# Two edits to a two-block kernel: 32 weight slots of the second block as three fp32r products, and the second norm's root moved behind the gate and up products

## The reference, cut to what matters

```python
# first block, each of 2 layers (D_FF = 2816)
h = h + jnp.concatenate([attn_out, conv_out], axis=-1) @ w_out[l]
hn = rmsnorm(h, norm2_g[l])
gate, up = jnp.split(hn @ w_gate_up[l], 2, axis=-1)
h = h + (jax.nn.silu(gate) * up) @ w_down[l]
...
# second block, one layer
h = _rms(x, g_mix) * (1.0 + sc1) + sh1
proj = h @ w_in     # gq gk gv gz gb ga | dil_q dil_k dil_v | gate_a gate_b
y_a = gated_deltanet(gq, gk, gv, gz, gb, ga, ...)
y_b = dilated_mixture(dil_q, dil_k, dil_v, ...)
merged = sigmoid(gate_a) * (y_a @ w_up_gdn) + sigmoid(gate_b) * (y_b @ w_up_dil)
x = x + gt1 * (merged @ w_out)
h2 = _rms(x, g_ffn) * (1.0 + sc2) + sh2
x = x + gt2 * moe_ffn(h2, ...)      # 64 experts, 8 for each token, and one shared
```

## Time and profile before

| | us |
|---|---|
| median of 3 runs | 1879.63 (1878.8 to 1880.18) |
| the profiled execution, its time | 1879.7 |
| its span in the trace | 1877.9 |
| TensorE busy | 1789.8 (95%) |
| VectorE busy | 826.2 (44%) |
| ScalarE busy | 595.0 (32%) |
| mean granted TensorE clock | 0.981 |

### The profile page before, as it was taken

How to read it: one execution, slowest core, us unless ns; L and a number is a source line. 1 busy time by engine, 2 the same in 40 slices (tenths; PEclk the granted TensorE clock), 3 DMA queues, 4 the chain that set the end, 5 groups by cost and what they waited for, 6 DMA issues and landing times.

```text
span 1877.9 us, 29645 instructions
## 1 busy us (share of the span) xinstructions
PE 1789.8 (95%) x11720; PEld 1392.1 (74%) x11720; DVE 826.2 (44%) x1587; ACT 595.0 (32%) x1100; POOL 55.7 (3%) x48
## 2 busy tenths in 40 slices
PE   7988999989989999799999999999999999999997
PEld 5767999977779999677888878887555555555554
DVE  4956555449666554376644373115222222222222
ACT  2244444311354443365521242203122222222221
POOL 0010000000010000005100000000000000000000
PEclk9999999999999999899999999998999999999999
DMA  6533445545344555332412323346799999999992
GB/s 271 220 125 146 139 176 179 181 154 203 138 161 151 181 188 194 115 123 92 130 46 90 122 103 112 134 148 241 277 392 395 399 396 402 395 398 398 391 401 98
DMA packets 63951, 403.97 MB, mean 215 GB/s; under 512 B 13056, under 2 KB 14592, under 8 KB 15232
## 3 DMA queue, kind: packets, MB, share of 16 engines
q1 hardware_dynamic: 63440, 401.34, 56.0%
q10 hardware_dynamic: 432, 1.51, 0.2%
HBM read 401.39 MB, written 1.44 MB: 215 GB/s over the span
## 4 chain that ended last, share of the span: by engine, by line
PE 87%; DVE 9%; ACT 3%; issue 1%; DMA 0%; SPq 0%; DVEq 0%; ACTq 0%
PE ps L826 22%; PE ps L1377 19%; PE ps L935 13%; PE ps L629 6%; PE ps L1351 5%; PE ps L1367 4%; DVE big L2098 2%; DVE inv L2321 2%; PE ps L1294 1%; PE ps L1268 1%; PE ps L585 1%; PE ps L1319 1%; PE ps L1277 1%; PE ps L1359 1%; PE ps L877 1%
## 5 line engine op out<-in xcount | busy, mean ns | idle before, releaser
L935 PE MATMUL ps<-hn,ring 128*128 128x256 f32 x1152 | 267.4, 385 | 3.6 <-ACT hn L1690 3.6
L935 PEld LDWEIGHTS ps<-hn,ring 128*128 128x128 f32 x1152 | 216.9, 193 | 36.4 <-issue 9.3
L826 PE MATMUL ps<-xhi,wlo 128*128 128x272 f32 (+1 forms) x800 | 227.5, 284 | 0.0
L826 PE MATMUL ps<-xhi,whi 128*128 128x272 f32 (+1 forms) x800 | 227.0, 284 | 0.0
L2161 DVE TENSOR_TENSOR wlo<-ring,whi 128x2048 fp32r<-128x2048 f32 x76 | 174.1, 2291 | 116.6 <-ACT whi L1560 116.6
L826 PE MATMUL ps<-hn_lo,whi 128*128 128x272 f32 (+1 forms) x672 | 192.3, 286 | 0.0
L1377 PE MATMUL ps<-big 128*64 128x512 f32 x816 | 181.8, 594 | 0.0
L1377 PE MATMUL ps<-ring,big 128*64 128x512 f32 x816 | 181.7, 594 | 0.0
L1560 ACT ACTIVATE whi<-ring 128x2048 fp32r<-128x2048 f32 x76 | 145.1, 1909 | 79.2 <-PE ps L826 78.8
L629 PE MATMUL ps<-hn,ring 128*128 128x272 f32 x640 | 159.3, 405 | 8.9 <-DVE hn L2069 5.6
L629 PEld LDWEIGHTS ps<-hn,ring 128*128 128x128 f32 x640 | 122.9, 195 | 41.3 <-issue 16.5
(11 more groups left out here) (399 smaller groups left out, 2628.9 us busy)
## 6 DMA issues: line engine op xcount, KB each, us to landing
ring<-in_stream SPq DMA_DIRECT2D x277, 1024.0 KB, 5.0
big<-in_stream SPq DMA_DIRECT2D x102, 1024.0 KB, 9.6
h<-in_xT SPq DMA_DIRECT2D x1, 1088.0 KB, 5.1
out_xT<-h SPq DMA_DIRECT2D x1, 1024.0 KB, 4.7
big<-in_consts ACTq DMA_DIRECT2D x1, 896.0 KB, 4.7
cst<-in_consts SPq DMA_DIRECT2D x1, 576.0 KB, 6.0
big<-in_consts ACTq DMA_DIRECT2D x1, 326.5 KB, 5.1
from_blocks<-big SPq DMA_DIRECT2D x1, 256.0 KB, 2.0
```

The source lines that it names most:

```text
L826: m = mm(out, a[:, at_:at_ + P], b[:, k, kept], start=first and i == 0, stop=last and i == 2)
L935: m = mm(ps[:, i % 2, n * T:(n + 1) * T], a, b, start=k == 0, stop=k == DC - 1)
```

## The change

It has two parts.

In the first block `normalize` is no longer called for the second norm. As each chunk of h gets w_out's result, VectorE multiplies it by the gain alone, ScalarE rounds it into `hg_hi` (a buffer of its own) and VectorE subtracts. TensorE still forms the sums of squares behind w_out (six chunks of squares, then two), then goes on to gate/up with the unscaled activation. VectorE multiplies both the gate and the up result by the reciprocal of the root, out of PSUM, for each of the 22 slots; ScalarE's silu then reads the scaled gate from SBUF.

In the second block the 32 slots from dq0 to UG3 are split like those of the first block: ScalarE rounds the slot into one of two buffers `wb` (`high_of`), VectorE subtracts into the ring of `wlo` (`low_of`), and each product is three fp32r matmuls. The activations `hm`, `yo` and `yb` are split as well; the low half of `hm` takes the place of `hm`. Buffers of the stretch move: the values of the dilated heads into pieces, `kbg`, `vn`, `sqy`, `dS` and `dpT` elsewhere. ScalarE's scaling of the keys for the state (`keys_scaled(gK, 96)`) moves from before the triangular inversion to behind it.

```diff
@@ TensorE, first block
-                    if c % 4 == 0:
-                        W(pe, "sq_ready", 2 * which + c // 4 + 1, l)
+                    if c in (0, 6 if which else 4):
+                        W(pe, "sq_ready", 2 * which + (c > 0) + 1, l)
...
@@ TensorE, second block
+            def both_of(name):
+                d = at(name) - SPLIT
+                W(pe, "wlo_ready", d + 1, DEPTH)
+                return wb[d % 2], wlo[(B2 + at(name)) % RING]
...
+                    pairs = [(hi, hm_hi), (lo, hm_hi), (hi, hm_lo)]
...
+                    for j, (w, x_) in enumerate(pairs):
+                        ...
+                        m = mm(ps[:, i % 2, n * T:(n + 1) * T], a, b, start=k + j == 0, stop=k == DC - 1 and j == len(pairs) - 1)
@@ ScalarE, first block
+                def high_part(c):
+                    W(act, "hn_ready", DC + c + 1, l)
+                    f(hg_hi[c][:, kept], hnf[:, c, kept], ACT.Copy).then_inc(xhi_ready, 1)
+                for n in range(3):
+                    high_weights(3 + n)
+                    high_part(2 * n)
+                    high_part(2 * n + 1)
+                f(sq[:, 0:6, kept], h[:, 0:6, kept], ACT.Square).then_inc(sq_ready, 1)
+                high_part(6)
+                high_part(7)
+                f(sq[:, 6:8, kept], h[:, 6:8, kept], ACT.Square).then_inc(sq_ready, 1)
                 root_of_mean(l, 1, small[:, 60:61])
-                for c in range(DC):
-                    W(act, "hn_ready", DC + c + 1, l)
-                    f(xhi[:, c, kept], hnf[:, c, kept], ACT.Copy).then_inc(xhi_ready, 1)
...
-                    f(sgu[:, i % 2, kept], ps[:, 2 * (i % 2), kept], ACT.Silu).then_inc(gate_act, 1)
+                    W(act, "gate_scaled", 2 * n + 1, l)
+                    f(sgu[:, i % 2, kept], sgu[:, i % 2, kept], ACT.Silu).then_inc(gate_act, 1)
@@ ScalarE, second block
+            def high_of(name):
+                i = ORDER.index(name)
+                act.wait_ge(ring_full[(B2 + i) % RING], ((B2 + i) // RING + 1) * 16)
+                if i == SPLIT:
+                    act.wait_ge(tu_full, 8)
+                elif i == SPLIT + 1:
+                    act.wait_ge(w_full, 4)
+                else:
+                    landed(ORDER[i - 2])
+                f(wb[(i - SPLIT) % 2][:, :], ring[:, (B2 + i) % RING, :], ACT.Copy).then_inc(whi_ready, 1)
...
@@ in dil_in(name), behind the copies (gate_out(j) likewise)
+                high_of(ORDER[i + 2])
@@ VectorE, first block
+                    W(dve, "h_added", 1 + n + 1, l)
+                    v.tensor_scalar(hnf[:, n, kept], h[:, n, kept], par[:, PN2 + n:PN2 + n + 1], None, ALU.mult).then_inc(hn_ready, 1)
...
-                normalize(l, 1, par[:, PN2:PN2 + DC], hnf)
...
+                    v.tensor_tensor(sgu[:, i % 2, kept], ps[:, 2 * (i % 2), kept], inv[:, 0, kept], ALU.mult).then_inc(gate_scaled, 1)
+                    v.tensor_tensor(up_r[i % 2][:, kept], ps[:, 2 * (i % 2) + 1, kept], inv[:, 0, kept], ALU.mult).then_inc(gate_scaled, 1)
@@ VectorE, second block
+            def low_of(name):
+                i = ORDER.index(name)
+                j = (B2 + i) % RING
+                W(dve, "whi_ready", i - SPLIT + 1, DEPTH)
+                v.tensor_tensor(wlo[j][:, :], ring[:, j, :], wb[(i - SPLIT) % 2][:, :], ALU.subtract).then_inc(wlo_ready, 1)
...
+            low_of("dk2")
             dil_norm("dq2")
             value_rest(2)
+            low_of("dv0")
             dil_norm("dk0")
             next_state(2)
+            low_of("dv1")
             dil_norm("dk1")
             value_rest(3)
...
             dil_weights(0)
+            low_of("ek0")
             dil_norm("eq0")
             dil_mask(1)
+            low_of("ek1")
             dil_norm("eq1")
             y_norm(1)
             dil_weights(1)
...
-            for d in range(4, 8):
-                dil_mask(d)
-                dil_weights(d)
+            low_of("G0")
+            dil_mask(4)
+            low_of("G1")
+            dil_weights(4)
+            low_of("G2")
+            dil_mask(5)
+            low_of("G3")
+            W(dve, "xhi_ready", 2, DEPTH)
+            v.tensor_tensor(yo_lo[:, :, :], yo, yo_hi[:, :, :], ALU.subtract).then_inc(xlo_ready, 1)
+            dil_weights(5)
+            low_of("G4")
+            low_of("G5")
+            dil_mask(6)
+            dil_weights(6)
+            low_of("G6")
+            low_of("G7")
+            dil_mask(7)
+            dil_weights(7)
```

More of the change, by code:

```diff
@@ L80 @@
 OUT2 = len(ORDER)
+SPLIT = ORDER.index("dq0")
 EX0 = B2 + OUT2 + 4
@@ L206, in build @@
         xhi, hn_lo, cat_lo, hff_hi, hff_lo = (rounded[n] for n in ("xhi", "hn_lo", "cat_lo", "hff_hi", "hff_lo"))
+        hg_hi = [rounded["hg_hi"][:, c, :] for c in range(DC - 1)] + [rounded["hg_hi7"][:, 0, :]]
+        up_r = [zpad[:, c, PAD:] for c in range(2)]
         ps = ctx.enter_context(nc.psum_tensor("ps", [P, 8, 512], F32))
@@ L295, in build @@
         flat = ps[:, :, :].rearrange("p a b -> p (a b)")
+        wb = [rounded[f"wb{j}"] for j in range(2)]
+        hm_hi, hm_lo = rounded["hm_hi"], xhi[:, :, 0:T]
+        yo_hi, yo_lo, yb_hi, yb_lo = (rounded[n] for n in ("yo_hi", "yo_lo", "yb_hi", "yb_lo"))
         COUNT = {}
@@ L825, in product @@
                     for i, (a, b) in enumerate(((w[0], hi), (w[1], hi), (w[0], lo))):
-                        m = mm(out, a[:, at_:at_ + P], b[:, k, kept], start=first and i == 0, stop=last and i == 2)
+                        b = b[k] if b is hg_hi else b[:, k, :]
+                        m = mm(out, a[:, at_:at_ + P], b[:, kept], start=first and i == 0, stop=last and i == 2)
                     return m
@@ L1259, in up_gdn @@
                 i, bank = at(name), UP_BANK[name]
-                w = slot(B2 + i, 0).rearrange("p (k n c) -> p k n c", k=8, n=2)
+                hi, lo = (w.rearrange("p (k n c) -> p k n c", k=8, n=2) for w in both_of(name))
                 if name == "UG0":
-                    pe.wait_ge(ya_ready, 4)
+                    W(pe, "xlo_ready", 2, DEPTH)
                     pe.wait_ge(mroot, len(SUMS))
@@ L1984, in _ @@
             dil_y_out(7)
+            act.wait_ge(yb_ready, 8)
+            f(yb_hi[:, :, :], yb, ACT.Copy).then_inc(xhi_ready, 1)
             act.dma_start(w_r, w_router_d).then_inc(loaded2, 16)
             act.dma_start(cst3, consts3_d).then_inc(loaded2, 16)
+            for name in ("UD0", "UD1", "UG2", "UG3"):
+                high_of(name)
             token_squares(2, lambda g: 8 + 4 * g + 4)
@@ L2525, in next_state @@
                 m.then_inc(s_ready, 1)
+            low_of("dq1")
             value_rest(0)
+            low_of("dq2")
             dil_norm("dq0")
             next_state(0)
+            low_of("dk0")
             value_rest(1)
+            low_of("dk1")
             dil_norm("dq1")
             next_state(1)
+            low_of("dk2")
             dil_norm("dq2")
             value_rest(2)
+            low_of("dv0")
             dil_norm("dk0")
             next_state(2)
+            low_of("dv1")
             dil_norm("dk1")
             value_rest(3)
+            low_of("dv2")
             dil_norm("dk2")
+            low_of("eq0")
+            low_of("eq1")
             dil_mask(0)
+            low_of("eq2")
             y_norm(0)
             dil_weights(0)
+            low_of("ek0")
             dil_norm("eq0")
             dil_mask(1)
+            low_of("ek1")
             dil_norm("eq1")
@@ L2553, in _ @@
             dil_weights(2)
+            low_of("ev1")
             dil_norm("ek1")
             dil_mask(3)
+            low_of("ev2")
             dil_norm("ek2")
@@ L2585, in _ @@
             merge(1)
+            low_of("UG3")
             times_dil(1)
```

118 lines of the change are left out of this document (72 added, 46 removed).

## The result

The changed kernel takes 1858.03 us (median of 4 runs, 1856.76 to 1858.69) against 1879.22 for the kernel before on the same chip (1877.32 to 1880.18). The ratio is 0.9888, with a 95% interval of 0.9871 to 0.9905: faster by 21.2 us where 18.6 were forecast, and inside the range of 1850 to 1871. The profiled execution took 1858.68 us, with a span of 1856.9.

The account below looks back on a forecast made before the run. TensorE was taken as the bound in the changed stretches, except eq0 to ev1, where it waits for VectorE; transfers set the pace in the last third. 1879.7 - 12.0 - 16.8 + 10.2 = 1861.1 us, range 1850 to 1871.

Parts of the forecast that it names:

- The first block's turn: From w_out to the second gate slot: waits and half clock go, gaining 6.5 us in layer 0, 5.5 in layer 1.
- Rival (d): First block: the first gate slot still waits for halves or squares, so only -6.6 us, 1873 us; chance 0.04.
- The scales at no cost: Gate/up loop: VectorE's iteration with the scales takes 5.45 us, fitting slots of 5.7 or 6.0 us; cost nothing.
- Rival (e): Gate/up loop: the scales make VectorE the bound, iterations over 6.3 us; slower, 1886 us at 6.6; chance 0.06.
- Slots of 5.7 us: Second block, dq0 to UG3: three fp32r products replace each fp32 one, 1.2 us less a slot, 38.4 over 32 slots.
- the walk: Second block: the three engines' queues followed from dq0 to UG3, giving a lead of 16.8 us before the clock's cost.
- The walk from eq0 to G7: Second block: longer TensorE waits for VectorE; lead 8.8 us at eq0, 5.1 at turn 3, 9.6 at UG0.
- Rival (b): Second block: waits shorter than in the walk and the clock stays up, 1851 us; chance 0.10.
- VectorE sets the pace: From eq0 to ev1: VectorE's work makes cycles of 22.8, 22.3 and 22.8 us; TensorE's shorter slots buy nothing.
- The clock: Second block: half clock behind TensorE's longer waits, counted as six at 1.7 us, costs 10.2 us.
- Rival (c): Second block: clock stays down as long as in layer 0, seven waits at 3.0 return 21 us, 1872; chance 0.14.
- The sum: Whole kernel: 1879.7 less 12.0 (first block) and 16.8 (second block), plus 10.2 (clock), gives 1861.1 us.

Follow-up runs that it names:

- the part alone: The kernel before with the first block's edits alone; 1871.35 us, ratio 0.9945.
- turns later: The changed kernel with each dil_turn one slot later in TensorE's order and dil_out(7) behind UG0; 1834.85 us, ratio 0.9775.
- weights first: The changed kernel with VectorE's dil_weights(d) ahead of y_norm(d), for d of 0 to 3; 1845.71 us, ratio 0.982.
- both orders changed: The changed kernel with VectorE's dil_weights ahead of y_norm and each dil_turn one slot later on TensorE; 1835.93 us, ratio 0.9778.
- the waits filled: The changed kernel with 164 useless fp32r products on TensorE ahead of dil_turn 0, 1, 2, 3 and 7; 1849.97 us, ratio 0.9841.

## Why the prediction was right

**The first block's turn: right, within 0.6 us.** The second slot comes 9.7 and 9.12 us after the sums began (9.8 and 9.5 expected), with no wait and the clock at 1.00. The gains at the place are 6.7 and 5.9, 12.6 in all, for 12.0, and the profile of the part alone shows the same two. That its times came to 10.3 only is put down to the scatter around them, which is not shown run by run. In the whole kernel the lead of 6.6 us had shrunk to 4.75 at layer 1's sums; behind the wait of 2.71 us in the unchanged norm that opens the layer, the low clock lasted longer than before, and the second profile of the same kernel, 1.9 us ahead at those sums, shows this as scatter. Rival (d) is out: no first slot waits.

**The scales at no cost: right, with the margin read too small.** The iteration takes 5.34 us, for 5.45. But "0.2 us to spare in layer 1" counted waits for ScalarE as part of VectorE's load: 1.0 us more per slot still fits. Rival (e)'s formula holds (11.1 against a measured 11.5 inside the two layers), but its condition lies much further off than 0.06 suggests, since work placed in the waits does not lengthen the iteration.

**Slots of 5.7 us: right.** The third window above has TensorE's nine slots in 87.9 us where they took 97.2: 9.3, less 0.3 for where the windows start, is the lead of 9.0 at eq0 that the walk had as 8.8. UG0 to UG3 take 34.7 us, for 34.2. The waits for value_rest are 1.37 and 1.48 (1.8 expected).

**The walk from eq0 to G7: right in each wait, a little high in the sum.** It had 3.5, 6.5, 5.4, 7.4, 2.4, 1.9 and 3.3 for what became 3.34, 6.25, 5.18, 7.10, 2.23, 1.52 and 3.09: 30.4 for 28.7. With the clock kept up, its cycle times are met within 0.3 us. Two of its sums do not come out as written: two waits of 1.8 us in place of 0.5 add 2.6 and not 2.3, and from turn 3 its terms (5.1 + 10.8 + 1.7 - 7.6) give 10.0 and not 9.6. In rival (e), 22 x 0.61 less 4 is 9.4. Rival (b), shorter waits with the clock up, is out.

**"VectorE sets the pace": only half right.** The sign to look for, over 90% busy from eq0 to ev1, was not there: 75.87 of 97.50 us, 78%, and 84 to 87% within the three cycles. Where the walk named VectorE's load, it was the two queues together: the turn stood so early on TensorE that it waited for VectorE, and the scores behind it then kept VectorE waiting. That the turns later alone are worth 21 us, as much as the whole change, is the proof; the load itself became the limit only then (98%).

**The clock: the mechanism right, the price with some luck.** 10.2 us stood in the sum for six waits at 1.7; five waits of 3.09 us or more cost 1.7 to 1.9 each, 8.9 in all. The price of 1.7 was that of the 3.68 us wait of before. Rival (c), which took layer 0's 3.0, did not come true in this kernel, but its price is found in this very stretch: behind waits of 4.72 and 5.61 us (weights first) and 3.21 us (turns later) the low clock lasted 5.6 to 6.1 us, so 2.8 to 3.0 were lost each time. The forecast had no reason that told the two cases apart, and no run here gives one. The Trainium skill, "TensorE: Matmul & The Clock Gate", on HAM oscillation, says that the cost comes back after each gap; the traces agree for each of the five long waits; behind those of 2.23 and 1.52 us they show no cost.

**The sum.** UG3 ended at 1230.5 us, for 1233.5. The first block's part had brought 11.4 by dq0, for 12.0. The second block was to give 16.8 less 10.2, 6.6 us, and gave 10.2. Against that stand 1.3 for the clock, 1.7 for the shorter turn waits and 0.8 for the two waits for value_rest, 3.8 together; 0.2 the other way are not placed. The mis-sized terms are thus the walk's waits, each 0.15 to 0.4 us too long (2.5 us), and then the clock's (1.3).

## What to carry to other kernels

When a slot gets cheaper on the engine that is the bound and dearer on another, walk both queues through one cycle and look at where each waits for the other: here eight calls moved by one slot gave as much again as the whole change. Here VectorE at 83%, and still waited for, was a question of order first; only at 98% was it one of work. And an added step is priced by the wait it lands in: three products of 0.34 us ahead of a 1.3 us wait were free, seven were not.

## What the runs showed of the hardware that was not expected

The length of the low stretch behind one and the same wait scatters. In the norm that opens layer 1, TensorE waits 2.71 and then 2.78 us in every profile, and the granted clock over 380 to 412 us was 0.84, 0.89, 0.95 or 1.00: 9.99, 8.54, 8.71 or 7.02 us from the first start to the second. That is up to 3 us of 1858, more than some edits are worth, so a term of a microsecond is not to be read from one profile of such a place. The start scatters as well: the versions of the changed kernel, alike up to there, reached layer 0's sums between 178.60 and 182.66 us.

No single length of wait decides whether the clock falls. In the second block it stayed at 1.00 behind waits of 2.23 (changed kernel), 2.60 and 2.73 us (turns later), and fell behind one of 2.56 (both orders changed; 0.72 over 1100 to 1106 us). One and the same wait goes both ways: turn 5's of 2.22 us had a low stretch behind it with the waits filled and with the weights first, and none in the changed kernel; the wait of 2.82 us of before had one, and with the first block's part alone, at 2.83 us, it had none. The clock fell behind every wait of 3.09 us or more, and stayed low for 2.8 to 6.1 us of the work that followed. Windows behind that turn 5 with the waits filled, behind the wait of 2.83 us with the first part alone, and behind those of 3.21 us (turns later) and 4.72 us (weights first):

```profile
1146.00:1152.00 6.00, 5.76 (x36) 5.76 (x37) 2.48 (x2) 2.29 (x2) 0.00 (x0) 0.72 0.37 153
```

```profile
1082.00:1088.00 6.00, 5.57 (x29) 5.01 (x30) 4.39 (x3) 1.20 (x2) 0.00 (x0) 1.00 0.17 71
```

```profile
1089.00:1096.00 7.00, 6.62 (x16) 4.30 (x17) 6.96 (x5) 3.49 (x5) 0.00 (x0) 0.54 0.21 89
...
1066.00:1073.00 7.00, 6.67 (x34) 6.67 (x35) 6.93 (x5) 1.95 (x3) 0.00 (x0) 0.55 0.01 2
```

Useless products in a wait are cheap: with 164 of them the kernel ran 8.8 us faster, 6.5 of it in the stretch where they stand.
